# Six buffers instead of four for the last weight pieces of a decoder step, and the sample's relus ahead of two weight splits

## The chip, the cores and the metric

The kernel runs on one core of a Trainium2 chip. The time is the device time of one execution in microseconds, lower is better; what is compared is the median of several runs of the kernel before and of the changed one. A profiled execution of the kernel before gives the trace that is read here.

## The reference

One decoder layer is applied to a prompt (512 tokens) and to a sample batch (8 sequences of 4 new tokens, so 32 rows, with 4096 cached tokens each). For this change only the last part matters: the output projection, the gated residual, and the squared-ReLU MLP with 1024 model columns and 4096 hidden columns, which prompt and sample both go through, each with its own modulation, and the final norm.

```python
def layer_out(x, attn, pool, mods, w_out, norm_mlp, w_up, w_down):
    _, _, g1, sh2, sc2, g2 = mods
    x = x + g1 * (jnp.concatenate([attn, pool], axis=-1) @ w_out)
    h = rms_norm(x, norm_mlp) * (1 + sc2) + sh2
    return x + g2 * (jnp.square(jax.nn.relu(h @ w_up)) @ w_down)
...
y_prompt = rms_norm(xp, norm_final)
y_sample = rms_norm(xs, norm_final)
```

All data are 32-bit floats.

## The kernel before

The program is written engine by engine, with semaphores and an order set by hand. The prompt's MLP is cut into eight chunks of 512 hidden columns. The loop over chunks runs beside the sample's attention over its eight sequences, one sequence per chunk, so that the cached keys and values stream in while TensorE does the prompt's products. The prompt's products are done in three passes: each weight and each activation is split into a high and a low part, so each quarter of a chunk's weights (512 KB) is loaded by SP (`load_up`, `load_down`), converted to its high part by ScalarE (`up_high`, `down_high`) and subtracted for its low part by POOL (`up_low`, `down_low`, line 706). `hidden` on ScalarE does relu, square and high part of a chunk's hidden rows, `hidden_low` on POOL their low part.

The sample's attention ends with the loop, so the sample's output projection and MLP come at the end, beside the prompt's last chunk (`LAST`, number 7). They read whole weight matrices once more, in pieces of 2 MB: pieces 0 and 1 are `w_out`, then piece 2 + 2i is columns 512 i to 512 i + 511 of `w_up` and piece 3 + 2i the matching rows of `w_down`, 18 pieces in all. `load_tail(n)` on SP issues piece n, `tail_slot(n)` is its buffer, `tail_lands(n)` the semaphore and count for which TensorE waits. Before, there are four buffers in turn (n mod 4): `mixT`, `W` slot 0, the lower half of `rw`, `W` slot 1. A buffer is free when the sample's product that read it is done (`sup_ps` counts the sample's up groups, `sdn_ps` its down groups). `hT` and the upper half of `rw` hold the prompt's normalized activations, low and high part, which the last up products of the prompt read until `up_ps` has reached `HP * LAST + 4`.

For one i the sample's chain is: `sample_up(i)` on TensorE (64 small products), a copy by VectorE (line 1529), `fold_up(i)` on TensorE (line 2109), `sample_relu(i)` on ScalarE (line 1035), a square on VectorE (line 1532 for i = 1, line 1540 otherwise), `sample_down(i)` on TensorE (64 small products). TensorE's order at the end is: the four up products of the prompt's last chunk with the sample's output projection, `sample_up(0)`, `fold_up(0)` and `sample_down(0)` between them; then `sample_up(1)`, most of `down(LAST, 0)`, `fold_up(1)`, most of `down(LAST, 1)`, `sample_down(1)` and the rest of both; then for i = 2, 3, 4 `sample_up(i)`, `down(LAST, 2i - 2)`, `fold_up(i)`, `down(LAST, 2i - 1)`, `sample_down(i)`; then for i = 5, 6, 7 `sample_up(i)`, `fold_up(i)`, the transposes for the prompt's final norm (`final_rows`), `sample_down(i)`. `down(LAST, 2q)` is the first to read quarter q of the down weights. Final norm on ScalarE and VectorE and the output rows on SP follow.

In SP's order before, pieces 4 and 5 are issued when the sample's output projection is done, then quarters 0 and 1 of the last down weights, piece 6, quarter 2, piece 7, quarter 3, and pieces 8 to 17 each when its buffer is free. On ScalarE the order is `hidden(LAST, 3)`, `down_high(LAST, 2)`, `down_high(LAST, 3)`, then the sample's relus from i = 1.

Of the kernel before, what the change touches and what calls it, by code (L numbers as in the profile page):

```python
# [129 lines left out]
def decoder_step(nc, x_prompt, x_sample, cache_k, cache_v, state_pool, page_table, c_prompt, c_sample, w_ada, b_ada,  # L130
# [4 lines left out]
    with ctx:  # L135
# [3 lines left out]
        def sem(name):  # L139
            return ctx.enter_context(nc.semaphore(name))  # L140
# [4 lines left out]
        def shared(suffix, dt, stack):  # L145
            sizes = (("hT", [P, FT, S]), ("gT", [P, HP, S]), ("kT", [P, HP, S]), ("rwT", [P, 2 * FT * S]),
                     ("W", [P, 4, 4096]), ("mixT", [P, FT, S]))
            return [stack.enter_context(nc.sbuf_tensor(name + suffix, shape, dt)) for name, shape in sizes]

        with ExitStack() as plain:  # L150
# [3 lines left out]
            hT, gT, kT, rw, W, mixT = shared("", F32, plain)  # L154
# [122 lines left out]
        def bank(i, parts=P, n=512, off=0):  # L277
            return PS[0:parts, i, off:off + n]


        def sems(names):
            return [sem(n) for n in names.split()]
# [5 lines left out]
        half_landed = sem("half_landed")  # L288
        w_landed = [sem(f"w_landed{i}") for i in range(4)]
        quarter_landed = [sem(f"quarter_landed{i}") for i in range(4)]  # L290
        tail_landed = [sem(f"tail_landed{i}") for i in range(4)]
        k_landed = [sem(f"k_landed{i}") for i in range(SLOTS)]
        v_landed = [sem(f"v_landed{i}") for i in range(SLOTS)]
        bias_out, bias_back, row_out, outs, y_out = sems("bias_out bias_back row_out outs y_out")
# [37 lines left out]
        sup_ps, srelu, ssqr, sdn_ps, xs_done = sems("sup_ps srelu ssqr sdn_ps xs_done")  # L332
# [31 lines left out]
        N_CH = FF // PIECE  # L364
# [24 lines left out]

        tail_slots = [mixT[:, :, :].rearrange("p a b -> p (a b)"), W[:, 0, :], rw[:, 0:4096], W[:, 1, :]]
        TAIL_SLOTS = len(tail_slots)

        N_TAIL = 2 + 2 * N_CH

        def tail_lands(n):

            return tail_landed[n % TAIL_SLOTS], 16 * (n // TAIL_SLOTS + 1)


        def tail_slot(n, cols=PIECE):
            return tail_slots[n % TAIL_SLOTS].rearrange("p (k n) -> p k n", n=cols)

# [5 lines left out]
        def down_quarter(b, q):  # L412
            return OUT_QUARTERS + 2 * PARTS * b + PARTS + q
# [4 lines left out]
        def down_part(q, memory=W, slot=RAW):  # L418
            return memory[:, slot, 1024 * q:1024 * q + 1024].rearrange("p (k n) -> p k n", k=HP)

        def rows_part(slot, q, memory=W):
            return memory[:, slot, 1024 * q:1024 * q + 1024]
# [12 lines left out]
        def in_bank(g):  # L435
            return (2, 3, 6, 7)[g] if g < 4 else 2 + g % 2
# [7 lines left out]
        def _(sp):  # L444
# [47 lines left out]
            def load_block(cache, ring, landed, b, j, freed=None):  # L492

                slot = j % SLOTS
                _, phys = nc.values_load_multi_w_load_instructions(pages[0:1, bass.ds(b * PAGES + PPB * j, PPB)],
                                                                   engines=[mybir.EngineType.SP])
                if freed:
                    sp.wait_ge(*freed)
                for pg in range(PPB):
                    sp.dma_start(ring[:, slot, pg, :], cache[bass.ds(phys[pg], 1), :, :].rearrange("a p n -> (a p) n"))\  # L500
                      .then_inc(landed[slot], 16)
# [13 lines left out]
            def load_down(b, q):  # L515

                sp.dma_start(down_part(q), wdown_d[bass.ds(b, 1), :, :, 2 * q * P:2 * (q + 1) * P]
                             .rearrange("a p k n -> (a p) k n")).then_inc(quarter_landed[q], 16)
# [9 lines left out]
            for m in range(FT):  # L528
                for n in range(4 * m, 4 * m + 4):
                    b, j = (SLOTS + n) // BLOCKS, (SLOTS + n) % BLOCKS  # L530
# [39 lines left out]
            def load_tail(n):  # L570
                i = n // 2 - 1
                if n < 2:
                    src, dst = wout_d[:, :, n * PIECE:(n + 1) * PIECE], tail_slot(n)
                elif n % 2 == 0:
                    src, dst = wup_d[:, :, i * PIECE:(i + 1) * PIECE], tail_slot(n)
                else:
                    src, dst = wdown_d[i, :, :, :], tail_slot(n, D)
                sp.dma_start(dst, src).then_inc(tail_landed[n % TAIL_SLOTS], 16)

            load_tail(0)  # L580
            for u in range(UNITS):
                section(LAST - 2, u, keys=u < 2)
                if u == 5:
                    sp.wait_ge(kt_ev, PAGES * DB)
                    load_tail(2)
                    sp.wait_ge(qk, UNITS * DB)
                    load_tail(1)
# [11 lines left out]
            load_tail(3)  # L599
            sp.wait_ge(so_ps, 1)  # L600
            load_tail(4)
            load_tail(5)
            sp.wait_ge(up_ps, HP * LAST + 1)
            load_down(LAST, 0)
            sp.wait_ge(up_ps, HP * LAST + 2)
            load_down(LAST, 1)
            sp.wait_ge(sup_ps, 1)
# [4 lines left out]
            load_tail(7)  # L612
            sp.wait_ge(up_ps, HP * LAST + 4)
            load_down(LAST, 3)
            for n in range(8, N_TAIL):
                sp.wait_ge((sup_ps, sdn_ps)[n % 2], (n - TAIL_SLOTS) // 2)
                load_tail(n)
            for t in range(TT):
                sp.wait_ge(fin_y, t + 1)
# [158 lines left out]
        def _(act):  # L778
# [52 lines left out]
            for g in range(16):  # L831
                act.wait_ge(proj_ps, g + 1)
                src = bank(in_bank(g))
# [126 lines left out]
            def hidden(b, m):  # L960

                act.wait_ge(up_ps, HP * b + m + 1)
                act.activation(kT[:, m, :], bank(5 + m % 2), ACT.Relu).then_inc(relu_ev, 1)  # L963
                act.wait_ge(relu_ev, HP * b + m + 1)
                act.activation(kT[:, m, :], kT[:, m, :], ACT.Square).then_inc(sqr_ev, 1)
                act.wait_ge(sqr_ev, HP * b + m + 1)
                act.activation(g_hi[:, m, :], kT[:, m, :], ACT.Copy).then_inc(g_high, 1)  # L967

            def down_high(b, q):

                act.wait_ge(quarter_landed[q], 16 * (down_quarter(b, 0) // PARTS + 1))
                act.activation(rows_part(HIGH, q, W_split), rows_part(RAW, q), ACT.Copy).then_inc(w_high, 1)  # L972
# [47 lines left out]
            def final_norm(t):  # L1020

                n = P if t < TT else NS
                act.wait_ge(fin_ps, t + 1)
                act.activation(junk[0:n, :], PS[0:n, 4 + 2 * (t % 2):6 + 2 * (t % 2), :].rearrange("p a b -> p (a b)"),
                               ACT.Square, accum_out=fstat[0:n, t, 0:1]).then_inc(fin_ss, 1)
                act.wait_ge(fin_ss, t + 1)
                act.activation(fstat[0:n, t, 1:2], fstat[0:n, t, 0:1], ACT.Sqrt, bias=eps[0:n, 0:1], scale=1.0 / D)\
                   .then_inc(fin_root, 1)

            def sample_relu(i):  # L1030

                act.wait_ge(sup_fold, i + 1)
                if i >= 2:
                    act.wait_ge(sdn_ps, i - 1)
                act.activation(gS[:, i % 2, :, :].rearrange("p a b -> p (a b)"), bank(1, P, HP * NS), ACT.Relu)\
                   .then_inc(srelu, 1)
# [11 lines left out]
            hidden(LAST, 2)  # L1048
            down_high(LAST, 1)
            hidden(LAST, 3)  # L1050
            down_high(LAST, 2)
            down_high(LAST, 3)
            for i in range(1, N_CH):
                sample_relu(i)
                if i == 5:
                    final_norm(0)
                    final_norm(1)
                elif i > 5:
                    final_norm(i - 4)
# [498 lines left out]
        def _(pe):  # L1558
# [508 lines left out]
            def piece_landed(n):  # L2067
                pe.wait_ge(*tail_lands(n))
# [138 lines left out]
```

## Time and profile before

| what | value |
|---|---|
| median of 3 runs | 892.75 us (888.73 to 893.92) |
| the profiled execution | 895.46 us |
| its span, first to last instruction | 893.5 us |
| mean granted TensorE clock | 0.978 |
| TensorE busy | 838.4 us, 94% of the span |
| VectorE, ScalarE, POOL busy | 50%, 38%, 33% |
| bytes moved by the DMA engines | 254.02 MB, 284 GB/s over the span |

Durations and waits are read from the trace of the profiled execution, in microseconds from the start of the span. A wait is put down to the instruction or transfer that ended it. "Landing" of a transfer is the time from its issue on SP to its completion.

### The profile page before, as it was taken

Reading aid. Unit: us, or ns where it says so; the run is one execution under the profiler, and the core shown is the slowest. Engines: PE = TensorE matmul, PEld = TensorE weight load, DVE = VectorE, ACT = ScalarE, POOL = GpSimd, SP = SyncE. Lnnn points to the kernel's source line nnn. Section 1 sums busy time; section 2 is a strip of 40 time slices with the busy share of each in tenths; the row PEclk is TensorE's granted clock in tenths of the full one; section 3 lists DMA queues with packets and bytes.
Section 4 is the critical chain, followed back from the end, with each engine's and each line's share of the span. In section 5 each row is a group of like instructions: output and inputs, shape, how many; then the busy total and the mean of one; then the engine's idle time right before and its main releaser. Section 6 shows DMA issues by size and latency. Waiting matters only on the chain.

```text
span 893.5 us, 20195 instructions
## 1 busy us (share of the span) xinstructions
PE 838.4 (94%) x7634; PEld 590.2 (66%) x7634; DVE 445.8 (50%) x845; ACT 338.5 (38%) x701; POOL 293.9 (33%) x191
## 2 busy tenths in 40 slices
PE   6799999898998799999999999999999999997984
PEld 4577786666766366666676676676676675575873
DVE  3643223774776784574674674674673541221222
ACT  4224213886123655236136036036036145133012
POOL 0330003856221354254334334334334353225000
PEclk9899999999998899999999999999999999999997
DMA  8942236597997579999999999899999999889896
GB/s 302 325 153 95 95 140 251 167 345 245 312 309 250 166 251 315 333 350 337 312 312 322 296 330 324 293 326 317 306 313 350 304 309 332 284 322 329 297 396 258
DMA packets 167825, 254.02 MB, mean 284 GB/s; under 512 B 10454, under 2 KB 69419, under 8 KB 167755
## 3 DMA queue, kind: packets, MB, share of 16 engines
q1 hardware_dynamic: 166995, 250.66, 82.7%
q0 software_dynamic: 768, 2.51, 0.8%
q8 instruction: 43, 0.70, 0.3%
q14 instruction: 19, 0.16, 0.1%
HBM read 248.56 MB, written 4.75 MB: 283 GB/s over the span
## 4 chain that ended last, share of the span: by engine, by line
PE 78%; DVE 7%; DMA 6%; ACT 3%; issue 2%; POOL 2%; SPq 1%; DVEq 0%; ACTq 0%
PE PS L1560 75%; POOL hT_split L644 2%; DMA mixT<-in_w_up_dram 2%; DMA W<-in_cache_v_dram 2%; DMA mixT<-in_x_prompt_dram 1%; DVE W L1337 1%; DMA W<-in_w_down_dram 1%; SPq L500 1%; PE PS L1909 1%; DMA W<-in_w_up_dram 1%; PE PS L1783 1%; ACT mixT L893 1%; DVE hT L1116 1%; DVE mixT L1277 1%; DVE xT L1405 1%
## 5 line engine op out<-in xcount | busy, mean ns | idle before, releaser
L706 POOL TENSOR_TENSOR W_split<-W,W_split 128x1024 fp32r<-128x1024 f32 x72 | 172.7, 2398 | 304.6 <-ACT W_split L866 141.8
L1560 PE MATMUL PS<-gT_split,W_split 128*128 128x512 f32 x576 | 201.0, 409 | 1.0 <-DVE xT L1405 0.2
L1337 DVE STREAM_TRANSPOSE W<-rwT 128x512 f32<-128x512 f32 x256 | 163.2, 683 | 61.2 <-DMA rwT<-in_cache_k_dram 35.1
L1560 PE MATMUL PS<-rwT_split,W_split 128*128 128x512 f32 x512 | 178.3, 409 | 5.3 <-POOL hT_split L644 5.2
L1560 PE MATMUL PS<-hT_split,W_split 128*128 128x512 f32 x416 | 163.2, 402 | 0.5 <-ACT mixT L939 0.5
L1560 PEld LDWEIGHTS PS<-gT_split,W_split 128*128 128x128 f32 x576 | 109.0, 189 | 53.8 <-issue 17.8
L1560 PEld LDWEIGHTS PS<-rwT_split,W_split 128*128 128x128 f32 x512 | 97.5, 190 | 40.4 <-issue 16.6
L866 ACT ACTIVATE W_split<-W 128x1024 fp32r<-128x1024 f32 x32 | 33.9, 1061 | 179.3 <-DMA W<-in_w_up_dram 179.3
L1560 PE MATMUL PS<-kT_split,W_split 128*128 128x512 f32 x256 | 100.0, 391 | 0.0
L1405 DVE SCALAR_TENSOR_TENSOR xT<-PS,mods,xT 128x512 f32<-128x512 f32 x64 | 47.2, 738 | 100.1 <-PE PS L1560 99.8
L1560 PEld LDWEIGHTS PS<-hT_split,W_split 128*128 128x128 f32 x416 | 79.6, 191 | 16.3 <-issue 1.6
L1560 PE MATMUL PS<-mixT_split,W_split 128*128 128x512 f32 x224 | 81.0, 404 | 2.5 <-POOL hT_split L644 2.5
L1560 PE MATMUL PS<-W,smp 128*32 128x512 f32 x512 | 71.9, 604 | 1.4 <-issue 0.8
L883 ACT ACTIVATE smp<-PS 32x128 f32<-32x128 f32 x256 | 68.9, 269 | 7.2 <-PE PS L1909 4.4
L1560 PEld LDWEIGHTS PS<-W,qcur 128*32 128x32 f32 x2048 | 52.8, 109 | 24.9 <-issue 20.2
L1560 PE MATMUL PS<-W,qcur 128*32 128x128 f32 x2048 | 69.1, 275 | 0.1
L721 POOL TENSOR_TENSOR kT_split<-kT,gT_split 128x512 fp32r<-128x512 f32 x32 | 43.5, 1361 | 64.9 <-ACT gT_split L967 64.8
L972 ACT ACTIVATE W_split<-W 128x1024 fp32r<-128x1024 f32 x32 | 33.8, 1057 | 52.3 <-DMA W<-in_w_down_dram 52.2
L1560 PEld LDWEIGHTS PS<-kT_split,W_split 128*128 128x128 f32 x256 | 48.2, 188 | 7.8
L1560 PEld LDWEIGHTS PS<-mixT_split,W_split 128*128 128x128 f32 x224 | 43.0, 192 | 15.0 <-issue 6.4
L963 ACT ACTIVATE kT<-PS 128x512 f32<-128x512 f32 x32 | 19.1, 598 | 66.7 <-PE PS L1560 66.5
L1560 PEld LDWEIGHTS PS<-W,smp 128*32 128x32 f32 x512 | 10.9, 108 | 28.2 <-issue 23.6
(273 smaller groups left out, 956.3 us busy)
## 6 DMA issues: line engine op xcount, KB each, us to landing
W<-in_cache_v_dram SPq DMA_DIRECT2D x256, 256.0 KB, 4.0
rwT<-in_cache_k_dram SPq DMA_DIRECT2D x256, 256.0 KB, 4.1
W<-in_w_ada_dram SPq DMA_DIRECT2D x12, 2048.0 KB, 10.0
W<-in_w_up_dram SPq DMA_DIRECT2D x32, 512.0 KB, 6.0
W<-in_w_down_dram SPq DMA_DIRECT2D x32, 512.0 KB, 5.7
W<-in_w_down_dram SPq DMA_DIRECT2D x8, 2048.0 KB, 9.8
rwT<-in_w_up_dram SPq DMA_DIRECT2D x4, 2048.0 KB, 10.4
mixT<-in_w_up_dram SPq DMA_DIRECT2D x4, 2048.0 KB, 11.8
```

Of the source, the lines that this page charges most:

```text
L500: sp.dma_start(ring[:, slot, pg, :], cache[bass.ds(phys[pg], 1), :, :].rearrange("a p n -> (a p) n"))\
L644: pool.tensor_tensor(h_lo[:, f, :], hT[:, f, :], high[:, f, :], ALU.subtract).then_inc(ready, 1)
L706: pool.tensor_tensor(rows_part(RAW, q, W_split), rows_part(RAW, q), rows_part(HIGH, q, W_split), ALU.subtract).then_inc(w_low, 1)
L721: pool.tensor_tensor(g_lo[:, m, :], kT[:, m, :], g_hi[:, m, :], ALU.subtract).then_inc(g_low, 1)
L866: act.activation(rows_part(HIGH, q, W_split), rows_part(RAW, q), ACT.Copy).then_inc(w_high, 1)
L883: last = act.activation(dst, src, ACT.Copy)
L893: act.activation(logits[s][:, 0:n], logits[s][:, 0:n], ACT.Exp, bias=stat[:, 0, s:s + 1], scale=-1.0, accum_out=stat[:, 1, s:s + 1]).then_ ...
L963: act.activation(kT[:, m, :], bank(5 + m % 2), ACT.Relu).then_inc(relu_ev, 1)
L972: act.activation(rows_part(HIGH, q, W_split), rows_part(RAW, q), ACT.Copy).then_inc(w_high, 1)
L1337: dve.transpose(ktb[u % 2][:, :, g, :], k_ring[:, j % SLOTS, pg, :]).then_inc(kt_ev, 1)
L1405: dve.scalar_tensor_tensor(xT[:, m, :], bank(5 + m % 2), mods[:, G2 + m, 0:1], xT[:, m, :], ALU.mult, ALU.add).then_inc(dn_ev, 1)
L1560: return pe.matmul(out, lhsT, rhs, start=start, stop=stop, **kw)
```

## The change

Three things are changed, all at the end of the program. There are six buffers for the weight pieces: `hT` and the upper half of `rw` are added, and a table gives each piece its buffer. Piece 8 and 9 go into the added buffers, and SP issues them right behind quarter 3 of the last down weights; from piece 10 on each is issued when the piece before it in its buffer has been used. Quarter 0 of the last down weights is issued ahead of piece 5. On ScalarE `sample_relu(1)` comes ahead of `down_high(LAST, 2)` and `sample_relu(2)` ahead of `down_high(LAST, 3)`.

```diff
-        tail_landed = [sem(f"tail_landed{i}") for i in range(4)]
+        tail_landed = [sem(f"tail_landed{i}") for i in range(6)]
...
-        tail_slots = [mixT[:, :, :].rearrange("p a b -> p (a b)"), W[:, 0, :], rw[:, 0:4096], W[:, 1, :]]
-        TAIL_SLOTS = len(tail_slots)
+        tail_slots = [mixT[:, :, :].rearrange("p a b -> p (a b)"), W[:, 0, :], rw[:, 0:4096], W[:, 1, :],
+                      hT[:, :, :].rearrange("p a b -> p (a b)"), rw[:, 4096:8192]]
+
+        TAIL_AT = (0, 1, 2, 3, 0, 1, 2, 3, 4, 5, 0, 1, 2, 3, 4, 5, 0, 1)
...
-            return tail_landed[n % TAIL_SLOTS], 16 * (n // TAIL_SLOTS + 1)
+            return tail_landed[TAIL_AT[n]], 16 * TAIL_AT[:n + 1].count(TAIL_AT[n])
...
-            return tail_slots[n % TAIL_SLOTS].rearrange("p (k n) -> p k n", n=cols)
+            return tail_slots[TAIL_AT[n]].rearrange("p (k n) -> p k n", n=cols)
...
-                sp.dma_start(dst, src).then_inc(tail_landed[n % TAIL_SLOTS], 16)
+                sp.dma_start(dst, src).then_inc(tail_landed[TAIL_AT[n]], 16)
...
             load_tail(4)
-            load_tail(5)
             sp.wait_ge(up_ps, HP * LAST + 1)
             load_down(LAST, 0)
+            load_tail(5)
...
             load_down(LAST, 3)
-            for n in range(8, N_TAIL):
-                sp.wait_ge((sup_ps, sdn_ps)[n % 2], (n - TAIL_SLOTS) // 2)
+            load_tail(8)
+            load_tail(9)
+            for n in range(10, N_TAIL):
+                before = n - 1 - TAIL_AT[n - 1::-1].index(TAIL_AT[n])
+                sp.wait_ge((sup_ps, sdn_ps)[n % 2], before // 2)
                 load_tail(n)
...
             hidden(LAST, 3)
+            sample_relu(1)
             down_high(LAST, 2)
+            sample_relu(2)
             down_high(LAST, 3)
-            for i in range(1, N_CH):
+            for i in range(3, N_CH):
                 sample_relu(i)
```

## Rows read from the trace of the kernel before

**Rows 1.** The page, part 2: GB/s moved in 40 equal slices.

```profile
GB/s 302 325 153 95 95 140 251 167 345 245 312 309 250 166 251 315 333 350 337 312 312 322 296 330 324 293 326 317 306 313 350 304 309 332 284 322 329 297 396 258
```

**Rows 2.** The chain that ended last, the end: start, us, what.

```profile
814.90 7.86 DMA W<-in_w_down_dram
...
861.82 15.06 DMA mixT<-in_w_up_dram
```

**Rows 3.** Timeline of ScalarE: start, us, line, operation, count, idle before and releaser.

```profile
802.44 1.06 ACT L972 ACTIVATE W_split<-W 128x1024 fp32r<-128x1024 f32 x1 [2.38 <-DMA W<-in_w_down_dram]
...
816.74 1.05 ACT L972 ACTIVATE W_split<-W 128x1024 fp32r<-128x1024 f32 x1
822.78 1.06 ACT L972 ACTIVATE W_split<-W 128x1024 fp32r<-128x1024 f32 x1 [5.00 <-DMA W<-in_w_down_dram]
823.75 0.26 ACT L1035 ACTIVATE gS<-PS 128x128 f32<-128x128 f32 x1
```

**Rows 4.** Timeline of TensorE's products, same columns.

```profile
818.86 0.27 PE L2109 MATMUL PS<-cst,smp 128*128 128x128 f32 x1
...
826.55 3.37 PE L1560 MATMUL PS<-W,gS 128*32 128x128 f32 x64 [5.34 <-DVE gS L1532]
...
836.19 0.27 PE L2109 MATMUL PS<-cst,smp 128*128 128x128 f32 x1
...
839.15 1.95 PE L1560 MATMUL PS<-W,gS 128*32 128x128 f32 x64
...
852.24 0.50 PE L1560 MATMUL PS<-gT_split,W_split 128*128 128x512 f32 x1
...
866.46 1.73 PE L1560 MATMUL PS<-rwT,hTs 128*32 128x128 f32 x55 [0.32 <-DMA rwT<-in_w_up_dram]
869.44 0.52 PE L1560 MATMUL PS<-rwT,hTs 128*32 128x128 f32 x9 [1.25 <-issue]
...
876.93 3.35 PE L1560 MATMUL PS<-mixT,hTs 128*32 128x128 f32 x64 [3.39 <-DMA mixT<-in_w_up_dram]
```

**Rows 5.** Windows: stretch, length, busy by engine (count), granted clock, DMA share, GB/s.

```profile
10.00:15.00 5.00, 3.90 (x14) 2.12 (x12) 1.91 (x4) 4.26 (x7) 0.00 (x0) 1.00 1.03 292
826.00:828.00 2.00, 1.45 (x28) 1.48 (x32) 0.41 (x1) 0.00 (x0) 0.26 (x1) 0.52 0.05 20
844.00:846.00 2.00, 2.00 (x11) 1.59 (x11) 0.16 (x1) 0.05 (x1) 0.00 (x0) 1.00 1.01 412
852.00:854.00 2.00, 2.00 (x20) 1.50 (x13) 0.29 (x1) 0.00 (x0) 0.00 (x0) 1.00 1.04 381
844.00:876.00 32.00, 27.12 (x520) 22.68 (x519) 9.12 (x17) 5.24 (x13) 0.00 (x0) 1.00 1.03 398
```

**Rows 6.** Timeline of VectorE, columns as in Rows 3.

```profile
824.04 2.37 DVE L1532 TENSOR_TENSOR gS<-gS 128x128 f32<-128x128 f32 x1 [6.93 <-ACT gS L1035]
...
837.05 0.28 DVE L1540 TENSOR_TENSOR gS<-gS 128x128 f32<-128x128 f32 x1
```

**Rows 7.** Timeline of POOL, columns as in Rows 3.

```profile
816.91 1.30 POOL L721 TENSOR_TENSOR kT_split<-kT,gT_split 128x512 fp32r<-128x512 f32 x1 [3.79 <-ACT gT_split L967]
...
823.92 2.34 POOL L706 TENSOR_TENSOR W_split<-W,W_split 128x1024 fp32r<-128x1024 f32 x1 [3.36 <-ACT W_split L972]
```

**Rows 8.** Line 578, pieces 8, 9, 16: issue ns, issue at; below it us to landing.

```profile
L578 SPq DMA_DIRECT2D mixT<-in_w_up_dram x1: 367/367/367, 816.8 to 816.8; - x1
...
DMA to landing us min/median/max: 11.2/11.2/11.2
...
L578 SPq DMA_DIRECT2D W<-in_w_down_dram x1: 367/367/367, 830.0 to 830.0; - x1
...
L578 SPq DMA_DIRECT2D mixT<-in_w_up_dram x1: 368/368/368, 861.8 to 861.8; - x1
...
DMA to landing us min/median/max: 15.1/15.1/15.1
```

**Rows 9.** Line 620, the first output row: issue ns, issue at.

```profile
L620 SPq DMA_DIRECT2D out_dram<-W x1: 4279/4279/4279, 866.6 to 866.6; - x1
```

## The prediction, made before the changed kernel was run

> **What bounds the kernel now.** I read the page first. TensorE is busy most of the span, but the slice row of bytes moved says that the end is another stage than the middle: 396 and 397 GB/s in two of the last four slices, against about 310 in the loop [rows 1]. So the end has to be read by itself, from the chain of what ended last. From 780 us on its two longest links off TensorE are transfers [rows 2]: the landing of a quarter of `w_down` (issued at 814.90, 7.86 us) and, much longer, the landing of a piece of `w_up` (issued at 861.82, 15.06 us). The reader should see two different stalls there, and ask of each which thing would be late next.
>
> The first stall is an order on ScalarE. After the last `hidden` it does `down_high(LAST, 2)` at 816.74, then stands 5.00 us until quarter 3 has landed, converts it at 822.78, and only then does `sample_relu(1)`, at 823.75 [rows 3]. TensorE had folded the sums for that relu at 818.86 to 819.13; it needs the squared relu for `sample_down(1)`, which starts at 826.55 after 5.34 us of idling and then runs its 64 matmuls in 3.37 us, where the same group takes 1.95 us at 839.15 [rows 4]. The granted clock around that is 0.52, about 1.2 of 2.4 GHz [rows 5]. Part of the stall is VectorE's square itself: 2.37 us at 824.04, where the same instruction takes 0.28 us at 837.05 [rows 6]; POOL's split of quarter 3 runs from 823.92 for 2.34 us, and the square ends with it [rows 7].
>
> The second stall is the weight stream. Piece 8 (the numbers of `load_tail`) is issued at 816.8 and lands 11.2 us later, at 828.0. Piece 9 needs the buffer of piece 5, which `sample_down(1)` frees, so it is issued only at 830.0 [rows 8]. Between them the queue is empty: 20 GB/s from 826 to 828. Once it has restarted the stream stays at 398 GB/s from 844 to 876 [rows 5], and from piece 14 on TensorE waits for landings: at 866.46 after 0.32 us of idling, at 876.93 after 3.39 [rows 4]. Piece 16, issued at 861.8, lands 15.1 us later, at 876.9 [rows 8]. So the end of the span is the time at which piece 16 lands, plus 16.6 us (893.5 - 876.9) of last sums, folds and final norm that the change leaves alone. The first stall costs TensorE time, but it reaches the end only because it also empties the stream.
>
> **The change, part by part.**
>
> *Relus earlier.* `sample_relu(1)` now waits only for the fold at 819.13. It takes 0.27 us and the square 0.28 to 0.29, so the product is ready at about 819.75, before TensorE asks for it at 821.2 (826.55 - 5.34). POOL is free at that moment: its hidden split starts at 816.91 and takes 1.30, and its next item, the low part of quarter 2, waits for a `down_high` that the relu now precedes. If POOL were busy all the same, the 2.37 us of [rows 6] would make it 821.8, a stall of 0.6. Gain on TensorE: 5.34 + (3.37 - 1.95) = 6.76, less 0 to 0.6; I take 6.7. What the move delays: `down_high(LAST, 2)` by 2.7 us (816.74 to 819.45), `down_high(LAST, 3)` behind `sample_relu(2)`, whose fold would be done at about 829.8 (836.19 + 0.27 before, less 6.7). Then 0.28 + 1.06 + 2.34 put the low part of quarter 3 at about 833.5; the first product that reads it, at 852.24 before [rows 4], starts at about 845.5. Twelve microseconds of cover: I cost it at nothing; were that cover gone, each microsecond of lateness would be one of TensorE's.
>
> *Quarter 0 ahead of piece 5.* ScalarE waited 2.38 us for quarter 0 and converted it at 802.44 [rows 3]. Now it lands before piece 5, by about 797, and is converted when the `hidden` before it ends, at 800.1. TensorE first reads it in `down(LAST, 0)`, behind the sample's second up group and with no wait ahead of it, so this gains nothing. Piece 5 moves back by a quarter's 1.3 us, to about 802.3, and is wanted at 821.2. SP's order past it is otherwise the same, `load_down(LAST, 1)` still waits for its own product. Nothing either way.
>
> *Six buffers.* Pieces 8 and 9 go to `hT` and the upper half of `rw`, free once the last up product is done (814.9), so SP issues them right after quarter 3, at 815.3 and 815.7, and piece 10 at 816.8. Piece 8 still lands at 828.0, since it queues behind piece 7 and quarter 3. But 9 and 10 follow without the hole, and from there each buffer's release comes well before its turn: piece 11 needs the end of `sample_down(1)` (823.2), 12 the end of `sample_up(2)`, 16 that of `sample_up(4)` (about 845.6), against data that would start at about 863. So the stream runs on from 828.0 at its own pace. At 398 GB/s a piece of 2.097 MB is 5.27 us, and eight more pieces put number 16 at 828.0 + 42.2 = 870.2. That is 6.7 us before 876.9. Bounds from the fastest and slowest rows of the full stream: 412 GB/s [rows 5] gives 5.09 a piece and 868.7 (8.2 gained), 381 GB/s gives 5.50 and 872.0 (4.9 gained). I take the row of 32 us, which averages them. SP may now stand in an issue: an output row issued behind three pieces took 4279 ns [rows 9]. Piece 10 may do so. That only happens with a full queue, and nothing but later pieces and, much later, the output rows stands behind it on SP, so I cost it at nothing.
>
> *The sum.* The two parts save the same 6 to 7 us, one on TensorE and one in the stream, and they don't add. TensorE alone would be ready for piece 16 at 873.54 (876.93 - 3.39), less 6.7 and less the 0.3 waited for piece 14: about 866.5. The stream brings it at 870.2. The later one counts: the stream. TensorE then stands about 3.6 us before `sample_up(7)`, as it stood 3.39, so that group's 3.35 us (low clock) and the 16.6 us behind it stay. The span becomes 893.5 - 6.7 = 886.8, the profiled execution 895.46 - 6.7 = 888.8. The median of the runs lies 2.7 below that execution, so the forecast is 892.75 - 6.7 = 886.1 us, bounds 884.6 to 887.9. Either part alone would bring most of it: with the relus alone piece 9 would be issued at 823.2, as piece 8's data run out; with the buffers alone TensorE would keep its stall and be ready for piece 16 at about 873.2, then run `sample_up(7)` in 1.95 instead of 3.37, some 5 us earlier than now. That makes the sign safer than the size.
>
> **The rivals.**
>
> 1. *The longer queue is slower.* In the old order at most about four transfers stand in the queue; now five or six do from 816 on. If a deep queue moved fewer bytes, the gain would go and turn: piece 16 comes later than 876.9 as soon as a piece takes over 6.1 us (48.9 / 8), below 343 GB/s. There is one full stretch like that: 292 GB/s at 10 to 15 us, with the first loads in flight at once [rows 5]; at that, 7.18 us a piece, piece 16 lands at 885.4 and the run takes 892.75 + 8.5 = 901.3. Against it: the 398 GB/s were reached with up to four transfers queued. Chance 0.04.
>  The Trainium skill points the same way: "DMA: Bandwidth & Descriptors", section Specifications, lists about 358 GB/s as what HBM gives one core. By that figure eight pieces would take 46.9 us, an estimated gain of 2.0 us instead of 6.7. The trace disagrees: 398 GB/s over 32 us, with one core running [rows 5].
> 2. *The pieces in the queue share it instead of following one another,* so that 16 lands with 17, at 828.0 + 9 x 5.27 = 875.4: a gain of 1.5, 891.2 us, the same within what is measurable. Against it: the starts at 866.46 and 876.93 are the landings of pieces 14 and 16, so 5.2 us for each piece, with several in the queue [rows 4]. Chance 0.09.
> 3. *TensorE comes late.* It had one hole of 1.25 us that the trace puts down to issue, in the middle of a group at 869.44 [rows 4]. More of these would first eat the 3.6 us in front of piece 16 at no cost. Four more would leave about 5 us of gain, eight more none. 888 to 892. Chance 0.06.
> 4. *The change doesn't do what it says:* the square still late, and the hole in the stream still there. Since either part closes the hole by itself, both must fail: 892.75. Chance 0.05.
> 5. *The stream runs better than its row* and TensorE sets the end: ready at 866.5, no wait and no low clock in `sample_up(7)`, up to 11.8 us, 881. That needs 435 GB/s; the best row has 412. Chance 0.03.
>
> **How the numbers follow.** The forecast keeps 0.73. About 0.5% (4.5 us) is what a measurement of this kernel can tell from no change, so faster means below 888.3. The forecast's bounds are all under that, but only just, and the three runs of before spread over 5.2 us, so about a tenth of its chance falls to "same". With rival 5: faster 0.68. Same: that tenth, rivals 2 and 4, and most of 3: 0.28. Slower: rival 1, 0.04. The range takes the bounds 884.6 to 887.9, some 1.5 us on both sides for the runs, and reaches up to rival 2 at 891.2 to hold 8 in 10: 882.8 to 891.2.
>
> **What would show it.** In the profile after: `sample_relu(1)` at about 819.2 and a square of 0.28 us; no idle time before `sample_down(1)`, its 64 matmuls in 1.95 us; pieces 8, 9 and 10 issued between 815 and 821 and no slice under 350 GB/s from 815 to 875; `sample_up(7)` at about 870, still behind a wait for its landing, and 16.6 us from there to the end. The forecast is wrong if the stream shows no hole and yet less than 380 GB/s (rivals 1, 2), or if `sample_up(7)` starts without waiting (rivals 3, 5).

## The result

The changed kernel takes 885.75 us (median of 8 runs, 883.57 to 890.48), the kernel before 892.59 (8 runs, 887.93 to 895.5). The ratio is 0.9933, 95% interval 0.991 to 0.9957: 6.0 us, between 3.8 and 8.0. The forecast was 886.1 and faster.

The runs of one kernel spread by some 7 us. SP issues quarter 3 of the last down weights at 814.90 in the trace of before, at 811.41 in that of after, and between 808.2 and 815.5 in those of the other kernels below. Two traces of the changed kernel itself have it at 811.41 and 814.81, and their spans differ by the same 3.4 us, all of it from ahead of the change. So the traces are compared by their *tail*: from that issue to the end of the span. It is 893.5 - 814.90 = 78.6 us before and 883.7 - 811.41 = 72.3 us after, 6.3 us less. The second profile of the changed kernel gave 72.3 again (887.1 - 814.81). One of the six runs of early_half_again, below, showed a lower granted clock and took 895.8 us, and its median leaves that run out.

The chain that ended last, in the changed kernel (start, us, what):

```profile
835.59 4.69 PE PS L1567 x76
840.28 0.02 issue
840.30 5.93 SPq L580
846.23 0.04 issue
846.27 19.89 DMA mixT<-in_w_up_dram
866.16 0.04 issue
866.21 3.60 PE PS L1567 x64
```

The landing of a quarter, which stood in [rows 2] at 814.90, is no longer in the chain. The landing of piece 16 still is, now with 5.93 us of SP standing in the issue ahead of it: the stream has become the chain from 840 on.

The first stall is gone. ScalarE, VectorE and POOL in the changed kernel (start, us, line, operation, count, idle before and releaser), against [rows 3, 6, 7]:

```profile
815.68 0.28 ACT L1040 ACTIVATE gS<-PS 128x128 f32<-128x128 f32 x1 [2.34 <-PE PS L2116]
815.86 1.05 ACT L977 ACTIVATE W_split<-W 128x1024 fp32r<-128x1024 f32 x1
```

```profile
815.99 0.29 DVE L1539 TENSOR_TENSOR gS<-gS 128x128 f32<-128x128 f32 x1 [2.36 <-ACT gS L1040]
```

```profile
813.42 1.29 POOL L726 TENSOR_TENSOR kT_split<-kT,gT_split 128x512 fp32r<-128x512 f32 x1 [3.80 <-ACT gT_split L972]
816.99 2.38 POOL L711 TENSOR_TENSOR W_split<-W,W_split 128x1024 fp32r<-128x1024 f32 x1 [2.28 <-ACT W_split L977]
```

The relu waits for the fold alone; the square falls into POOL's idle 2.28 us and takes 0.29 instead of 2.37. TensorE, the same columns, against [rows 4]:

```profile
817.66 1.95 PE L1567 MATMUL PS<-W,gS 128*32 128x128 f32 x64
...
859.11 0.52 PE L1567 MATMUL PS<-hT,hTs 128*32 128x128 f32 x9 [1.72 <-issue]
...
866.21 3.55 PE L1567 MATMUL PS<-mixT,hTs 128*32 128x128 f32 x64 [3.11 <-DMA mixT<-in_w_up_dram]
...
876.18 1.75 PE L2139 MATMUL PS<-cst,xTs 128*32 128x128 f32 x8 [0.98 <-DVE xTs L1561]
```

`sample_down(1)` follows without a wait, in 1.95 us. TensorE still stands 3.11 us for piece 16, and the group behind that wait still takes 3.55 us. The hole in the stream is gone too (windows: stretch, length, busy by engine with counts, granted clock, DMA share, GB/s):

```profile
798.00:800.00 2.00, 2.00 (x52) 1.59 (x54) 0.00 (x0) 0.00 (x0) 2.00 (x1) 1.00 0.22 77
822.00:824.00 2.00, 2.00 (x44) 1.67 (x37) 0.29 (x1) 0.00 (x0) 0.00 (x0) 1.00 1.05 410
812.00:872.00 60.00, 53.82 (x971) 44.85 (x966) 14.01 (x28) 9.81 (x22) 6.04 (x3) 0.97 1.04 398
```

The 20 GB/s of [rows 5] lay 11 us behind the issue of quarter 3; that place is at 822 here, with 410 GB/s, and the 60 us from 812 hold 398, the rate of [rows 5]. An older hole, ahead of piece 6, stays (77 GB/s at 798).

SP in the changed kernel (start, us in the issue):

```profile
811.83 0.51 SPq L580 DMA_DIRECT2D hT<-in_w_up_dram  x1
812.38 1.82 SPq L580 DMA_DIRECT2D rwT<-in_w_down_dram  x1
814.24 3.67 SPq L580 DMA_DIRECT2D mixT<-in_w_up_dram  x1
819.67 6.15 SPq L580 DMA_DIRECT2D W<-in_w_down_dram  x1
...
846.27 2.84 SPq L580 DMA_DIRECT2D mixT<-in_w_up_dram  x1
```

Their landings, pieces 8 and 16 (issue ns, issue at, and below it us to landing), against [rows 8]:

```profile
L580 SPq DMA_DIRECT2D hT<-in_w_up_dram x1: 509/509/509, 811.8 to 811.8; - x1
...
DMA to landing us min/median/max: 12.2/12.2/12.2
...
L580 SPq DMA_DIRECT2D mixT<-in_w_up_dram x1: 2838/2838/2838, 846.3 to 846.3; - x1
...
DMA to landing us min/median/max: 19.9/19.9/19.9
```

Pieces 8, 9 and 10 are issued right behind quarter 3. From piece 9 on SP stands in its issues, up to 6.5 us in one.

### The profile page after: what moved, and what is told of

Read it like the earlier page. It is cut to its first block, busy times and chain, and to the rows that moved or that the text cites. A ratio compares the mean times of both kernels' runs of the same rounds, so it can differ in the third digit from the quotient of the medians.

```text
span 883.7 us, 20195 instructions
## 1 busy us (share of the span) xinstructions
PE 837.1 (95%) x7634; PEld 588.8 (67%) x7634; DVE 442.1 (50%) x845; ACT 337.5 (38%) x701; POOL 293.8 (33%) x191
## 4 chain that ended last, share of the span: by engine, by line
PE 79%; DMA 7%; DVE 6%; ACT 2%; SPq 2%; issue 2%; POOL 1%; DVEq 0%; ACTq 0%
PE PS L1567 76%; DMA mixT<-in_w_up_dram 2%; DMA W<-in_cache_v_dram 2%; POOL hT_split L649 1%; DMA W<-in_w_ada_dram 1%; DMA mixT<-in_x_prompt_dram 1%; DVE W L1344 1%; SPq L502 1%; PE PS L1916 1%; SPq L580 1%; DMA W<-in_w_up_dram 1%; PE PS L1790 1%; DVE hT L1123 1%; DVE xT L1412 1%; DVE mixT L1284 0%
## 5 line engine op out<-in xcount | busy, mean ns | idle before, releaser
L1567 PEld LDWEIGHTS PS<-rwT_split,W_split 128*128 128x128 f32 x512 | 97.7, 191 | 40.5 <-issue 16.6
```

Source lines behind the costliest of these rows:

```text
L1567: return pe.matmul(out, lhsT, rhs, start=start, stop=stop, **kw)
```

## The experiments

Ratios are against the kernel before, run in the same session; the tail is that of the one profiled execution.

| kernel | median us | ratio (95% interval) | tail us |
|---|---|---|---|
| before | 892.59 | | 78.6 |
| changed | 885.75 | 0.9933 (0.991 to 0.9957) | 72.3 |
| relus_only | 886.36 | 0.9937 (0.9907 to 0.9967) | 73.0 |
| buffers_only | 888.6 | 0.9978 (0.9952 to 1.0004) | 76.7 |
| quarter_only | 891.13 | 1.0002 (0.998 to 1.0023) | 77.0 |
| relu_one | 885.12 | 0.9915 (0.9883 to 0.9946) | 72.7 |
| relu_between | 883.59 (1 run) | | 72.2 |
| half_stream | 880.26 | 0.9871 (0.9834 to 0.9907) | 65.4 |
| buffers_half | 888.56 | 0.9951 (0.9924 to 0.9978) | 73.4 |
| twice_up | 888.32 | 0.9943 (0.9924 to 0.9962) | 74.0 |
| early_half | 884.16 | 0.9912 (0.9879 to 0.9946) | 70.7 |
| changed_again | 886.34 | 0.9929 (0.9896 to 0.9961) | 72.3 |
| early_half_again | 882.83 | 0.9892 (0.9847 to 0.9937) | 70.0 |

**The parts one by one.** The theory on trial is the prediction's: the stream sets the end, and either part closes its hole. First the relus alone, with four buffers and SP's old order:

```diff
             hidden(LAST, 3)
+            sample_relu(1)
             down_high(LAST, 2)
+            sample_relu(2)
             down_high(LAST, 3)
-            for i in range(1, N_CH):
+            for i in range(3, N_CH):
```

> Four buffers and the old order of the loads, only the two relus moved. Theory (the stream sets the end, and either part closes its hole): piece 9 is issued some 6.8 us earlier, about 8.3 us behind the issue of quarter 3 instead of 15.1, just as piece 8's data run out; about 0.5 us of hole stays; 6.2 us less than the kernel before, so about 886.4. Rival T (TensorE sets the end): 6.7 us less, the whole of the change. Rival D (the buffers do it): 1 us or less. Size of the stall before sample_down(1): 0.

SP and TensorE in relus_only:

```profile
812.97 0.37 SPq L517 DMA_DIRECT2D W<-in_w_down_dram  x1
814.88 0.37 SPq L578 DMA_DIRECT2D mixT<-in_w_up_dram  x1
821.23 0.37 SPq L578 DMA_DIRECT2D W<-in_w_down_dram  x1
```

```profile
868.33 3.64 PE L1562 MATMUL PS<-mixT,hTs 128*32 128x128 f32 x64 [3.43 <-DMA mixT<-in_w_up_dram]
```

Piece 9 is issued 8.3 us behind quarter 3, as expected, and that is enough: no hole is left where half a microsecond was expected (403 GB/s from 824 to 830), and the tail shrinks by 5.6 of the 6.3 us, the ratio is nearly that of the whole change. TensorE waits 3.43 us for piece 16, so here too the stream is what comes last. Rival D falls; T's extra half microsecond can't be told apart by the time.

Then the buffers alone, with quarter 0 ahead of piece 5 (the changed kernel with ScalarE's old order):

```diff
             hidden(LAST, 3)
-            sample_relu(1)
             down_high(LAST, 2)
-            sample_relu(2)
             down_high(LAST, 3)
-            for i in range(3, N_CH):
+            for i in range(1, N_CH):
```

> Six buffers and quarter 0 ahead of piece 5, the relus left behind the two splits. Theory: the stall before sample_down(1) stays at about 5.3 us with the slow 64 products behind it, the stream has no hole, piece 16 lands about 42 us behind piece 8, TensorE comes about 3 us later than it and sample_up(7) starts without a wait at the full clock; 5.1 us less than before, about 887.5. Rival T (TensorE sets the end): no gain, 892.6. Rival S (the stream alone, TensorE never): the whole 6.7 us.

TensorE in buffers_only:

```profile
819.52 3.25 PE L1565 MATMUL PS<-W,gS 128*32 128x128 f32 x64 [4.83 <-DVE gS L1537]
...
862.55 0.51 PE L1565 MATMUL PS<-hT,hTs 128*32 128x128 f32 x9 [2.05 <-issue]
...
865.56 2.44 PE L1565 MATMUL PS<-rwT,gS 128*32 128x128 f32 x64
867.82 1.48 PE L1565 MATMUL PS<-mixT,hTs 128*32 128x128 f32 x45
871.09 0.85 PE L1565 MATMUL PS<-mixT,hTs 128*32 128x128 f32 x19 [1.79 <-issue]
```

Half right. The stall stays and no landing is waited for behind it, as expected: TensorE comes after the stream here. But the gain is 1.9 us of tail (2.0 by the ratio), not 5.1. The missing 3 us stand in the rows: two holes in the middle of the sample's up groups, 2.05 and 1.79 us, put down to issue, and a low clock behind the first (0.55 from 863 to 865; `sample_down(6)` takes 2.44 us instead of 1.95). The prediction had allowed for one hole of 1.25, the one in [rows 4]; the second, in `sample_up(7)`, does not show where TensorE waits for piece 16 ahead of it. Rival T, no gain at all, is not excluded: the ratio's interval reaches 1.0004, and a tail 1.9 us shorter is hardly more than the 1.6 us by which that of quarter_only, next, is shorter at an equal time. So a gain of the buffers alone is likely and not shown.

Quarter 0 ahead of piece 5, alone:

```diff
             load_tail(4)
-            load_tail(5)
             sp.wait_ge(up_ps, HP * LAST + 1)
             load_down(LAST, 0)
+            load_tail(5)
```

> Only quarter 0 ahead of piece 5, all else as before. Theory: nothing, 892.6, since TensorE first reads quarter 0 some 14 us after it has landed either way; down_high(LAST, 0) starts some 2 us earlier on ScalarE and piece 5 lands about 1.3 us later. A rival that has this order as part of the gain: 1.3 us less or more.

No change in time, 1.0002. Its one profile has a tail 1.6 us shorter than before all the same: there the clock had fallen one group earlier (0.68 in `sample_down(6)`), `sample_up(7)` waited only 1.53 us for piece 16, which landed 0.7 us sooner behind quarter 3's issue, and ran at the full clock in 1.95 us instead of 3.35. So one tail is good to some 1.6 us where the clock's turn is involved, and the time decides.

The second relu put back:

```diff
             sample_relu(1)
             down_high(LAST, 2)
-            sample_relu(2)
             down_high(LAST, 3)
+            sample_relu(2)
```

> The changed kernel with sample_relu(2) left behind down_high(LAST, 3); only sample_relu(1) comes ahead of the splits. Theory (only the first relu mattered, since quarter 3 has landed long before the second one's fold is done): as the changed kernel, tail 72.3 us; the split of quarter 3 starts some 3.5 us earlier. Rival (both relus carry the gain): a stall before sample_down(2), and 1 us more or above.

ScalarE in relu_one:

```profile
814.60 1.05 ACT L977 ACTIVATE W_split<-W 128x1024 fp32r<-128x1024 f32 x1
817.57 1.06 ACT L977 ACTIVATE W_split<-W 128x1024 fp32r<-128x1024 f32 x1 [1.92 <-DMA W<-in_w_down_dram]
824.94 0.28 ACT L1040 ACTIVATE gS<-PS 128x128 f32<-128x128 f32 x1 [6.31 <-PE PS L2116]
```

Quarter 3 is converted at 817.57, 7.5 us earlier behind its issue than in the changed kernel (3.5 were expected), and the second relu waits another 6.31 us for its fold: its place makes no difference, and no stall appears. The gain is that of the first relu.

**What sets the end.** Take work from the stream:

```diff
+                if n >= 10:
+                    part = FT // 2 if n % 2 == 0 else HP // 2
+                    src, dst = src[:, 0:part, :], dst[:, 0:part, :]
                 sp.dma_start(dst, src).then_inc(tail_landed[TAIL_AT[n]], 16)
```

> The changed kernel with pieces 10 to 17 loaded by half (the first half of their rows of the contraction only; the other half of the buffer keeps what lay there), the products as they were. Theory (the stream sets the end of the changed kernel): TensorE no longer waits for a landing; the 3.1 us ahead of sample_up(7) go, and its 64 products take 1.95 us instead of 3.55; 4.7 us less than the changed kernel, about 881.0. Rival T (TensorE or the chain behind it sets the end): as the changed kernel, 885.75. A stream whose time did not scale with its bytes: also 885.75.

TensorE in half_stream:

```profile
853.75 1.93 PE L1570 MATMUL PS<-hT,hTs 128*32 128x128 f32 x64
...
858.99 1.93 PE L1570 MATMUL PS<-mixT,hTs 128*32 128x128 f32 x64
```

5.5 us less than the changed kernel (880.26 against 885.75; 6.9 in the tail), a little more than the 4.7 expected. The waits for landings are gone, and both up groups run through at the full clock in 1.93 us; only the last transposes are slow (1.89 us at 0.50). Most of the rest is the hole in `sample_up(6)`, which is gone as well. So the stream sets the end of the changed kernel, and rival T falls.

Give work to TensorE:

```diff
-                for k in range(FT):
-                    for g in range(QUADS):
...
+                for _ in range(2 if i in (2, 3, 4) else 1):
+                    for k in range(FT):
+                        for g in range(QUADS):
```

> The changed kernel with the 64 products of sample_up(2), (3) and (4) done twice, with the same result: 5.3 to 5.8 us more work for TensorE, all ahead of the last pieces. Theory (the stream sets the end, TensorE has 3.1 us to spare before piece 16 and loses another 1.6 to the low clock behind that wait): the wait before sample_up(7) goes, its products run at the full clock, 0.8 us more than the changed kernel, up to 2.6 if a hole in sample_up(7) comes to light. Rival T (TensorE sets the end): 5.5 us more, 891.2.

TensorE in twice_up:

```profile
837.73 2.16 PE L1567 MATMUL PS<-hT,hTs 128*32 128x128 f32 x68 [1.11 <-issue]
...
860.10 1.93 PE L1567 MATMUL PS<-rwT,hTs 128*32 128x128 f32 x64
...
872.05 0.74 PE L1567 MATMUL PS<-rwT,gS 128*32 128x128 f32 x18 [0.86 <-issue]
...
872.63 2.01 PE L1567 MATMUL PS<-mixT,hTs 128*32 128x128 f32 x61
```

The added products brought two holes of their own, 1.11 and 1.12 us, so TensorE came later than the 5.5 us of the expectation: `sample_up(5)` starts 46.3 us behind quarter 3's issue (860.10 - 813.77), in the changed kernel 38.1 (849.50 - 811.41). Of these 8.2 us 1.7 reach the tail, and 0.001 the ratio (about 0.9 us), inside the 0.8 to 2.6 of the theory. `sample_up(7)` follows its predecessor without a wait and at the full clock. What TensorE had to spare is what the prediction counted, the wait of 3.11 us for piece 16 and the 1.6 us of low clock behind it, and besides the hole of 1.72 us in `sample_up(6)`, which is not there in twice_up: 6.4 us.

Start part of the stream earlier. Half of piece 8 goes into parts of `scn` and `smp` that are free once the attention is done, behind quarter 1:

```diff
             load_down(LAST, 1)
+            for h in range(2):
+                cols = slice((EARLY // 2 - 1) * PIECE, EARLY // 2 * PIECE)
+                sp.dma_start(early[h], wup_d[:, 2 * h:2 * h + 2, cols]).then_inc(early_landed, 16)
...
+                if n == EARLY:
+                    src, dst = src[:, 4:FT, :], dst[:, 4:FT, :]
                 sp.dma_start(dst, src).then_inc(tail_landed[TAIL_AT[n]], 16)
```

> The changed kernel with the first half of piece 8 (1 MB) loaded into parts of scn and smp that are free by then, right behind quarter 1 of the last down weights, so that it fills half of the hole that the stream has ahead of piece 6. Theory (the stream sets the end): everything behind quarter 3 lands 2.6 us earlier, the wait before sample_up(7) shrinks from 3.1 to about 0.5 us; 2.6 us less than the changed kernel, up to 4.2 if the clock then stays up; about 882.8. Rival T (TensorE sets the end): no change, 885.75.

Windows, then TensorE, in early_half:

```profile
798.00:800.00 2.00, 2.00 (x42) 1.57 (x44) 0.41 (x1) 1.34 (x2) 1.53 (x2) 1.00 1.04 363
860.00:862.00 2.00, 1.72 (x9) 1.54 (x9) 0.52 (x2) 0.28 (x1) 0.00 (x0) 0.65 1.06 391
```

```profile
859.30 0.60 PE L1575 MATMUL PS<-hT,hTs 128*32 128x128 f32 x10 [1.78 <-issue]
...
862.15 2.82 PE L1575 MATMUL PS<-rwT,gS 128*32 128x128 f32 x64
864.80 1.48 PE L1575 MATMUL PS<-mixT,hTs 128*32 128x128 f32 x44
867.50 0.85 PE L1575 MATMUL PS<-mixT,hTs 128*32 128x128 f32 x20 [1.22 <-issue]
```

The older hole is filled where it was (363 GB/s at 798), and no landing is waited for any more. Piece 16 lands 52.4 us behind quarter 3's issue instead of 54.8. But the gain is 1.6 us of tail, not 2.6 or more: TensorE has become the last, with its two holes of 1.78 and 1.22 us and a group at the low clock between them. Once more, beside the changed kernel:

> The changed kernel once more, beside the two that follow: 0.993 of the kernel before. Its tail, from the issue of quarter 3 to the end of the span, was 72.3 us in the first profile (78.6 before); the same again within 1 us.

> The changed kernel with the first half of piece 8 loaded early, once more beside the changed kernel. The first run gave 0.991, against 0.993. Theory (the stream comes earlier, and what then sets the end is TensorE, with its two holes of 1.2 to 1.8 us): 1.6 us less than the changed kernel, tail 70.7 us, and no wait for a landing ahead of sample_up(7). Rival (the difference was chance): as the changed kernel.

The tails were 72.3 and 70.0 us, the ratios 0.9929 and 0.9892. Both times early_half came out ahead of the changed kernel, by 1.9 and 3.3 us in the ratios and by 1.6 and 2.3 us in the tails. The intervals of the ratios overlap, so against the changed kernel it is likely and not settled; against the kernel before it is clear, about 1%.

**The holes in TensorE's groups.** buffers_only with its pieces 10 to 17 loaded by half, as in half_stream:

> buffers_only with pieces 10 to 17 loaded by half (the first half of their rows of the contraction only). In buffers_only no landing is waited for behind sample_down(1), but TensorE stands twice in the middle of a sample's up group, 2.05 and 1.79 us, put down to issue. Theory H (TensorE's instructions come late while the stream is full): both holes go, 3.8 us less than buffers_only, about 884.8 (0.992 of before). Rival N (no landing is waited for, so the halved stream changes nothing): as buffers_only, 888.6 (0.998). The stall before sample_down(1) stays in both.

TensorE in buffers_half:

```profile
860.25 1.93 PE L1568 MATMUL PS<-hT,hTs 128*32 128x128 f32 x64
...
867.62 0.85 PE L1568 MATMUL PS<-mixT,hTs 128*32 128x128 f32 x19 [0.64 <-issue]
```

In the trace theory H holds: the hole of 2.05 us is gone, that of 1.79 is 0.64, together 3.2 us less, and the tail is 3.3 us shorter than in buffers_only, though no landing was waited for there. The time is not as clear: the ratio went from 0.9978 to 0.9951, 2.4 us, with overlapping intervals, and the medians are equal. So that a full stream delays TensorE's instructions is shown by the traces of two pairs (changed and half_stream, buffers_only and buffers_half), while its price in the time is not settled. What it delays is told in the last section.

**VectorE beside POOL.** The relu between the two splits:

```diff
             hidden(LAST, 3)
-            sample_relu(1)
             down_high(LAST, 2)
+            sample_relu(1)
             sample_relu(2)
```

> The changed kernel with sample_relu(1) between down_high(LAST, 2) and down_high(LAST, 3) instead of ahead of both. The relu still comes right behind the fold, but POOL's split of quarter 2 now runs at that moment. Theory (VectorE's square of two operands in SBUF stands while POOL works): the square takes 1.1 to 1.3 us instead of 0.29 and ends with POOL's split, some 0.5 us before TensorE asks for it, so no stall and no change in time. Rival (the 2.37 us of the kernel before had another cause): 0.29 us as in the changed kernel.

VectorE, then POOL, in relu_between:

```profile
814.21 1.23 DVE L1539 TENSOR_TENSOR gS<-gS 128x128 f32<-128x128 f32 x1 [2.36 <-ACT gS L1040]
```

```profile
812.89 2.40 POOL L711 TENSOR_TENSOR W_split<-W,W_split 128x1024 fp32r<-128x1024 f32 x1
```

The square takes 1.23 us and ends at 815.44, POOL's split at 815.29. With the 2.37 us of [rows 6] and the 0.29 of the changed kernel these are three lengths of one instruction, and the two long ones end 0.15 us behind POOL's split. The Trainium skill's "Trainium Architecture — The Big Picture", section What this means for kernel authors, says that the port pair shared by VectorE and GpSimd is "an exclusive lock (not a bandwidth split)"; the trace agrees, 1.23 against 0.29 us. TensorE did not wait, and the tail is 72.2.

## Why the prediction was right, and where it was not

*The sum.* Right in mechanism and size. The tail of the forecast was 78.6 - 6.7 = 71.9 us; it is 72.3, and the medians differ by 6.8. That the forecast and the median lie 0.35 us apart is luck: the gain is only known to lie between 3.8 and 8.0. Its two ends moved as follows. Piece 16 landed 62.0 us behind the issue of quarter 3 before (876.9 - 814.9) and 54.8 after (866.2 - 811.4): 7.2 us earlier, where 6.7 were forecast. The stream's rate was the one chosen: piece 8 landed at 824.0 and piece 16 at 866.2, eight pieces in 42.2 us, 5.27 each. The half microsecond more came from piece 8, which landed 12.6 us behind quarter 3's issue instead of 13.1. Against that the part behind piece 16 was not left alone, as the prediction had it: 17.5 us instead of 16.6 (883.7 - 866.2), 0.2 in `sample_up(7)` and 0.6 in the last transposes, which took 1.75 us; both ran at the low clock (0.53 and 0.55). In the kernel before the transposes had been faster (TensorE, at 0.88):

```profile
886.68 1.12 PE L2132 MATMUL PS<-cst,xTs 128*32 128x128 f32 x8 [0.98 <-DVE xTs L1554]
```

*The opening reading* of [rows 1] is wrong in one value: of the last four slices one has 396 GB/s, the others 329, 297 and 258. That the end is a stage of its own rests on the 398 GB/s of [rows 5], and nothing in the sum uses the slices.

*Relus earlier.* Right in each number: relu right behind the fold, square 0.29, no stall, 1.95 us. That a busy POOL lengthens the square, for which 0.6 us of stall were allowed, relu_between shows: 1.23 us, and still no stall. Costing the later `down_high(LAST, 3)` at nothing was right, and relu_one shows that with six buffers the second relu need not have been moved at all.

*Quarter 0 ahead of piece 5.* Nothing, as costed: 1.0002.

*Six buffers.* The stream ran on without the hole, as said. Wrong was the picture of the queue: by the landings about four pieces were under way at a time, not "five or six". SP stood in its issues, and piece 16, which could have been issued at about 842, was issued at 846.3 and landed 19.9 us later, so that about 3.8 pieces (19.9 / 5.27) lie between an issue and its landing. That cost nothing, as the prediction held for a standing SP. It also means that the deeper queue of rival 1 never came about.

*"Either part alone would bring most of it."* This step failed for one of the two. The relus alone brought 5.6 of 6.3 us, where 6.2 of 6.7 were said; the buffers alone 1.9 at most, where 5 were said, and even that is not told from nothing. The mis-sized term is rival 3's: the hole of 1.25 us was taken as one and as covered. There are two, 2.05 and 1.79 us in buffers_only, with a low clock between them, and they are covered only where TensorE waits for the stream anyway. In the changed kernel they are, so the sum did not suffer. The added buffers are worth about 0.7 us of tail on top of the relus (73.0 to 72.3), which the time can't tell from nothing.

*The rivals.* 1 and 2 (a slower queue, a shared queue) fall by the 398 GB/s and the 5.27 us. The Trainium skill ("DMA: Bandwidth & Descriptors", section Specifications) lists a limit of about 358 GB/s for what HBM gives a core; the trace disagrees, with 398 GB/s over 60 us. 3 was the one with something in it, as just told. 4 fell by the traces. 5 is what half_stream made true by other means: 5.5 us more to be had by a shorter stream.

## What to carry to other kernels

Where an engine's stall also empties a queue that the end depends on, look for the cheapest edit that ends the stall: here two activations (with six buffers one was enough) moved ahead of two others, of which the second waits for data, brought nearly the whole gain, and two more buffers hardly added to it. Two edits that close the same hole don't add up, and what each is worth alone depends on what is late next; so find the second-latest thing before crediting either. Compare traces over the stretch that was changed, from an event ahead of it: two traces of the changed kernel have the same tail within 0.1 us, two of early_half within 0.7, with spans more than 3 us apart each time.

## What the runs showed of the hardware

- TensorE stood in the middle of groups of small products, with nothing waited for: one to four such holes at the end of every trace but half_stream's, 18 in all. Counted over all of TensorE's instructions, weight loads and products included, they all lie at the 49th or 50th of a stretch of 256: behind the 55th product of `sample_up(6)` in eight traces, 127 products (some 254 loads and products) further on in buffers_only and buffers_half, behind the 54th in early_half, which has one instruction more ahead of it, and elsewhere in twice_up, whose added products shift the count. The small groups between the prompt's large products, `sample_up(2)` to `sample_up(5)` in the changed kernel, have none. The Trainium skill's "Runtime: NRT & Kernel Launch", section Instruction fetch mechanics, says that instructions are refilled in blocks of 256, which agrees with that distance, and that the fetch is hidden by the pace of issue, which does not agree with these holes. The traces have the refills, as transfers of 16 KB on a DMA queue of their own; here is that queue over the whole span (packets, MB, share), in the changed kernel and in twice_up with its 384 more loads and products:

```profile
q8 instruction: 43, 0.70, 0.3%
```

```profile
q8 instruction: 44, 0.72, 0.3%
```

Each of the 18 holes ends 1.3 to 1.5 us behind the landing of one of these transfers. In the changed kernel the transfer from 856.6 to 857.7 starts 3.8 us after TensorE has passed the place before, beside a stream of 405 GB/s, and the hole ends at 859.11. In half_stream, whose stream runs dry there (0 GB/s from 853 to 855), the same transfer starts 1.2 us after that place, and there is no hole. The holes are 0.86 to 2.05 us long with the stream at 341 to 419 GB/s, and 0.64 and 0.62 us with it down at 0 and 26 (buffers_half, twice_up). So a full stream holds up the refill; no run changed the refill itself.

- SP can be kept in an issue: up to 6.5 us in the changed kernel and 7.5 in relu_between, with about four 2 MB transfers under way. In the kernel before, where piece 16 landed 15.1 us behind its issue (2.9 pieces), no issue of a piece from 8 on took more than 0.37 us.
- A wait of 3.1 to 3.4 us ahead of 64 small products made them nearly twice as long (3.35 to 3.64 us instead of 1.95, at a granted clock of 0.50 to 0.55, so near 1.2 GHz). So a wait at the end cost 1.4 to 1.7 us more than itself. Where the wait was 1.53 us (quarter_only) they kept 1.95, at 1.00. But holes of 1.7 to 2.05 us, with the shorter waits for the fold behind them, also brought the clock down: to 0.64 over the next 2 us in quarter_only, 0.65 in early_half and 0.55 in buffers_only. Behind the 1.72 us of the changed kernel it stayed at 1.00.
